# Retention in a streaming encoder step: queries times state in two rounded parts and three passes; one value buffer, queries and keys tile by tile in three slots

## The reference, cut to what matters

```python
def step(r, qkv):
    qc, kc, vc = qkv
    qf, kf, vf = qc.astype(F32), kc.astype(F32), vc.astype(F32)
    s = jnp.einsum('bihd,bjhd->bhij', qf, kf) * intra[None]
    o = jnp.einsum('bhij,bjhe->bihe', s, vf)
    o = o + jnp.einsum('bihd,bhde->bihe', qf, r) * q_dec
    r = r * c_dec + jnp.einsum('bjhd,bjhe->bhde', kf * k_dec, vf)
    return r, o.astype(vc.dtype)
...
o = head_norm(o, gn_g.reshape(RET_HEADS, RET_DV)).reshape(b, L, RET_VW) * jax.nn.silu(g)
return x + gate[:, None, :] * (o @ w_out), r
```

## Time and profile before

| | us |
|---|---|
| median of 3 runs (1730.53 to 1733.26) | 1731.53 |
| the profiled execution, its own time | 1732.81 |
| its span, first to last instruction | 1731.0 |

### The profile page before, as it was taken

How to read it: one execution, slowest core, us unless ns; L and a number is a source line. 1 busy time by engine, 2 the same in 40 slices (tenths; PEclk the granted TensorE clock), 3 DMA queues, 4 the chain that set the end, 5 groups by cost and what they waited for, 6 DMA issues and landing times.

```text
span 1731.0 us, 22378 instructions
## 1 busy us (share of the span) xinstructions
PE 1677.8 (97%) x8585; PEld 1344.3 (78%) x8585; DVE 766.0 (44%) x1588; ACT 559.6 (32%) x926; POOL 380.9 (22%) x501
## 2 busy tenths in 40 slices
PE   3999999999999999999999999999999999999998
PEld 2899997777876766667668888888788876888987
DVE  4664443212244454545543333665553106654442
ACT  4221121111133435434440223523322125444442
POOL 2111111211133334333322223414211010110000
PEclk7999999999999999999999999999999999999999
DMA  9545545563456767677663312222322726343201
GB/s 309 182 146 175 186 143 194 177 219 130 166 165 203 241 185 237 181 224 241 201 234 113 110 42 89 95 98 75 96 91 86 219 92 197 128 118 103 74 25 37
DMA packets 137004, 260.75 MB, mean 151 GB/s; under 512 B 16931, under 2 KB 60095, under 8 KB 136898
## 3 DMA queue, kind: packets, MB, share of 16 engines
q1 hardware_dynamic: 104114, 167.23, 30.6%
q0 software_dynamic: 32784, 92.08, 15.6%
HBM read 178.83 MB, written 80.43 MB: 150 GB/s over the span
## 4 chain that ended last, share of the span: by engine, by line
PE 84%; DVE 5%; issue 2%; ACT 2%; DMA 2%; POOL 1%; SPq 0%; DVEq 0%; POOLq 0%
PE trunk_ps L1120 34%; PE in_ps_o L537 12%; PE in_ps_o L533 11%; PE tail_ps L2040 6%; PE tail_ps L2031 4%; PE tail_ps L1998 3%; PE trunk_ps L1163 3%; PE trunk_ps L1147 3%; PE tail_ps L2008 2%; PE tail_ps L1966 1%; DVE room L1558 1%; PE in_ps_o L558 1%; PE trunk_ps L1158 1%; POOL room L1428 1%; PE trunk_ps L1223 1%
## 5 line engine op out<-in xcount | busy, mean ns | idle before, releaser
L1120 PE MATMUL trunk_ps<-w_hi,hT_hi 128*128 128x512 f32 x1008 | 412.3, 409 | 0.6 <-DVE w_lo L210 0.6
L1120 PE MATMUL trunk_ps<-w_hi,hT_lo 128*128 128x512 f32 x1008 | 399.3, 396 | 0.0
L1120 PE MATMUL trunk_ps<-w_lo,hT_hi 128*128 128x512 f32 x1008 | 398.0, 395 | 0.0
L1120 PEld LDWEIGHTS trunk_ps<-w_hi,hT_hi 128*128 128x128 f32 x1008 | 189.7, 188 | 60.7 <-issue 17.5
L1120 PEld LDWEIGHTS trunk_ps<-w_lo,hT_hi 128*128 128x128 f32 x1008 | 189.9, 188 | 48.1 <-issue 5.0
L1120 PEld LDWEIGHTS trunk_ps<-w_hi,hT_lo 128*128 128x128 f32 x1008 | 189.5, 188 | 46.3
L210 DVE TENSOR_TENSOR w_lo<-w_raw,w_hi 128x1024 fp32r<-128x1024 f32 x76 | 96.5, 1271 | 114.3 <-ACT w_hi L198 108.7
L533 PE MATMUL in_ps_o<-hT_hi,w_hi 128*128 128x384 f32 x384 | 130.6, 340 | 0.4 <-DVE hT_lo L664 0.4
L533 PE MATMUL in_ps_o<-hT_hi,w_lo 128*128 128x384 f32 x384 | 129.1, 336 | 0.0
L533 PE MATMUL in_ps_o<-hT_lo,w_hi 128*128 128x384 f32 x384 | 129.0, 336 | 0.0
L537 PE MATMUL in_ps_o<-w_hi,hT_hi 128*128 128x512 f32 x288 | 114.4, 397 | 0.0
(11 more groups left out here) (256 smaller groups left out, 2854.6 us busy)
## 6 DMA issues: line engine op xcount, KB each, us to landing
w_raw<-in_a_w_in SPq DMA_DIRECT2D x96, 256.0 KB, 3.4
room<-in_state_ret SPq DMA_DIRECT2D x64, 256.0 KB, 4.3
out_state_sample<-room POOLq DMA_DIRECT2D x64, 256.0 KB, 6.8
room<-in_b_ada_w SPq DMA_DIRECT2D x24, 512.0 KB, 6.7
scratch_qkT<-room POOLq DMA_DIRECT2D x48, 192.0 KB, 2.2
scratch_v_hi<-room POOLq DMA_DIRECT2D x36, 256.0 KB, 2.6
scratch_v_lo<-room POOLq DMA_DIRECT2D x36, 256.0 KB, 3.1
scratch_o<-room POOLq DMA_DIRECT2D x36, 256.0 KB, 3.4
```

Of the source, the lines that this page charges most:

```text
L1120: ins = pe.matmul(ps[:, bank, :], h[:, k, t * P:(t + 1) * P], w[:, (C0 + j) % 2, k, :], start=k + m == 0, stop=k == KT - 1 and m == 2)
```

## The change: what it does

1. The query-state product of tiles 1 to 7 is made of six fp32r matmuls (three for each half of the state) in place of two fp32 ones. Their operands are made one tile ahead: ACT rounds the state and the next tile's queries behind the scaling of the output, POOL makes the state's low part ahead of the gating, DVE the queries' low part behind the coefficients and ahead of `half_low` and `split_lo`.
2. Values have one buffer: POOL issues the load for tile n + 1 right after output n, ahead of the state's low part.
3. Queries and keys come tile by tile (256 KB each) into a ring of three slots, each freed by the scores and by the query's low part (or by the copy for the strips).
4. The semaphores of a few memory clears and of the last head's row loads are merged; buffers move.

```diff
-        qk = [at(9216, 4, NB3), at(11776, 4, NB3)]
+        qk = [at(9216 + 4 * P * i, 4, P) for i in range(3)]
...
+        def qk_landed(h, c):
+            g = score_no(h, c)
+            return qk_in[g % 3], 16 * (g // 3 + 1)
...
             def load_qk(g):
...
+                h, c = g // T, order[g % T]
+                if g >= 3:
+                    ph, pc = (g - 3) // T, order[(g - 3) % T]
+                    sp.wait_ge(scored, g - 2)
+                    if pc == SELF:
                         sp.wait_ge(qs_ready, ph + 1)
+                    elif pc:
+                        sp.wait_ge(q_split, 7 * ph + pc)
...
+                src = dr["qkT"][4 * h:4 * h + 4, :, c * P:(c + 1) * P].rearrange("a p t -> p a t")
+                sp.dma_start(qk[g % 3], src).then_inc(qk_in[g % 3], 16)
...
+                    if T * h + t + 4 < T * RH:
+                        load_qk(T * h + t + 4)
...
             def output(h, c):
...
                 if c:
-                    pe.wait_ge(state_new, n)
-                    q, _ = qk_of(h, c)
+                    pe.wait_ge(q_split, 7 * h + c)
+                    pe.wait_ge(state_split, 7 * h + c)
                     for a in range(2):
-                        ins = pe.matmul(ps[:, PS_O, :], q[:, a, :], state[:, a, :], start=False, stop=a == 1)
+                        for m, (q, r_) in enumerate(((q_hi, state_hi), (q_hi, state_lo), (q_lo, state_hi))):
+                            ins = pe.matmul(ps[:, PS_O, :], q[:, a, :], r_[:, a, :], start=False, stop=a == 1 and m == 2)
...
                     act.activation(o_t, ps[:, PS_STR if t == SELF else PS_O, :], ACT.Identity, bias=sc[:, 2:3], scale=sc[:, 1:2]).then_inc(o_scaled, 1)
+                    if t + 1 < PT:
+                        act.wait_ge(state_new, PT * h + t + 1)
+                        act.copy(state_hi[:, :, :], state[:, :, :]).then_inc(hi_made, 1)
+                        act.wait_ge(*qk_landed(h, t + 1))
+                        act.copy(q_hi, qk_of(h, t + 1)[0]).then_inc(hi_made, 1)
                     if t % 2 and t < 2 * SUBS:
...
             def load_v(n):
...
-                if n >= 2:
-                    ph, pc = divmod(n - 2, PT)
+                if n:
+                    ph, pc = divmod(n - 1, PT)
                     pool.wait_ge(o_done, ph * T + pc + 1)
...
+            def state_low(h, c):
+
+                pool.wait_ge(hi_made, 14 * h + 2 * c + 1)
+                pool.tensor_tensor(state_lo[:, :, :], state[:, :, :], state_hi[:, :, :].bitcast(F32), ALU.subtract).then_inc(state_split, 1)
...
+                    if t < PT and PT * h + t + 1 < RH * PT:
+                        load_v(PT * h + t + 1)
+                    if t + 1 < PT:
+                        state_low(h, t)
                     pool.wait_ge(g_evac, n + 1)
                     pool.wait_ge(o_scaled, n + 1)
                     pool.tensor_tensor(o_t, o_t, g_t[:, :], ALU.mult).then_inc(gated, 1)
...
-                    if t < PT and 8 * h + t + 2 < RH * PT:
-                        load_v(8 * h + t + 2)
...
+            def query_low(h, c):
+
+                dve.wait_ge(hi_made, 14 * h + 2 * c)
+                dve.tensor_tensor(q_lo, qk_of(h, c)[0], q_hi.bitcast(F32), ALU.subtract).then_inc(q_split, 1)
...
                     coefficients(n)
+                    if t + 1 < PT:
+                        query_low(h, t + 1)
                     if h == RH - 1:
                         half_low(t, 1)
```

More of the change, by code:

```diff
@@ L773, in trunk @@
         part = lambda o, n: pr.parts[:, o:o + n]
-        v_hi, v_lo = (part(o, 2 * DV).rearrange("p (a b) -> p a b", a=2) for o in (0, 2 * DV))
-        k_hi, k_lo = part(4 * DV, DK), part(4 * DV + DK, DK)
-        s_hi, s_lo = part(4 * DV + 2 * DK, P), part(4 * DV + 2 * DK + P, P)
+        v_hi, v_lo = part(0, DV), part(DV, DV)
+        k_hi, k_lo = part(2 * DV, DK), part(2 * DV + DK, DK)
+        s_hi, s_lo = part(2 * DV + 2 * DK, P), part(2 * DV + 2 * DK + P, P)
+        state_hi, state_lo = pr.state_hi, pr.state_lo
+        q_hi, q_lo = pr.q_parts[:, 0], pr.q_parts[:, 1]
         vs = at(6912, DV)
@@ L808, in trunk @@
         ps_t = ps[:, 4:8, :].rearrange("p (a b) c -> p a b c", a=2)
-        qk_in = [sem(f"qk_in{i}") for i in range(2)]
-        v_in = [sem(f"v_in{i}") for i in range(2)]
+        qk_in = [sem(f"qk_in{i}") for i in range(3)]
+        v_in, hi_made, q_split, state_split = sem("v_in"), sem("hi_made"), sem("q_split"), sem("state_split")
         parted = sem("parted")
@@ L815, in trunk @@
         o_stored = [sem(f"o_stored{i}") for i in range(2)]
-        orow_in = [sem(f"orow_in{i}") for i in range(2)]
         vs_in, cols_in, p_stored = sem("vs_in"), sem("cols_in"), sem("p_stored")
-        scored, decayed, s_ready, qs_clear, qs_ready = sem("scored"), sem("decayed"), sem("s_ready"), sem("qs_clear"), sem("qs_ready")
+        scored, decayed, s_ready, cleared, qs_ready = sem("scored"), sem("decayed"), sem("s_ready"), sem("cleared"), sem("qs_ready")
         upd, o_done, state_new, strips_done, strip_new = sem("upd"), sem("o_done"), sem("state_new"), sem("strips_done"), sem("strip_new")
@@ L892, in score_no @@
             return h * T + order.index(c)
[L894 to L897, removed]
+        def qk_landed(h, c):
+            g = score_no(h, c)
+            return qk_in[g % 3], 16 * (g // 3 + 1)
         def qk_of(h, c):
-            _, buf, at_ = portion_of(h, c)
-            cut = slice(at_ * P, (at_ + 1) * P)
-            return qk[buf][:, 0:2, cut], qk[buf][:, 2:4, cut]
+            slot = qk[score_no(h, c) % 3]
+            return slot[:, 0:2], slot[:, 2:4]
         def strip_tile(t):
@@ L967, in orow_load @@
                     sp.wait_ge(half_turned, 2 * t + half - 1)
[L968 removed]
+                sp.dma_start(orow[half], dr["o"][t * P:(t + 1) * P, half * CW:(half + 1) * CW]).then_inc(o_in[half], 16)
             def o_rows(i):
@@ L1195, in half_turn @@
             def half_turn(t, half):
-                pe.wait_ge(orow_in[half], 16 * (t + 1))
+                pe.wait_ge(o_in[half], 16 * (t + 1))
                 if t + half:
@@ L2305, in build @@
             under.enter_context(nc.sbuf_tensor("under_room", [P, 4096], F32))
-            pr.parts = under.enter_context(nc.sbuf_tensor("parts", [P, 4 * DV + 2 * DK + 2 * P], F32R))
+            pr.parts = under.enter_context(nc.sbuf_tensor("parts", [P, 2 * DV + 2 * DK + 2 * P], F32R))
+            pr.state_lo = under.enter_context(nc.sbuf_tensor("state_lo", [P, 2, DV], F32R))
+        with ExitStack() as under:
+            under.enter_context(nc.sbuf_tensor("under_queries", [P, 11776], F32))
+            pr.q_parts = under.enter_context(nc.sbuf_tensor("q_parts", [P, 2, 2, P], F32R))
+            pr.state_hi = under.enter_context(nc.sbuf_tensor("state_hi", [P, 2, DV], F32R))
         room = acts.enter_context(nc.sbuf_tensor("room", [P, ROOM], F32))
```

54 lines of the change are left out of this document (16 added, 38 removed).

## The result

| | before | changed kernel |
|---|---|---|
| median of 5 runs, us | 1731.53 (1728.71 to 1733.47) | 1804.26 (1800.35 to 1808.62) |
| profiled execution, us | 1732.81 | 1800.35 |
| its span, us | 1731.0 | 1798.5 |
| ratio of the medians, 95% interval | | 1.0424 [1.0400, 1.0448] |

What follows compares the result with a forecast made beforehand. TensorE, busy almost throughout, bounds the kernel; every second retention tile it waits for ACT, then DVE. -9.4 + 41.6 + 12 + 9.1 + 6 = +59 us on 1732.8 gave 1792, 1791 as a median; range 1752 to 1812.

Steps and rivals of the forecast that it cites:

- passes: Query-state product, tiles 1 to 7 of four heads: six rounded passes replace two fp32 matmuls, saving 9.4 us.
- splitting: Making high and low parts on ACT, POOL and DVE delays TensorE in retention: 41.6, 9.1 and 6 us.
- strips: Tiles 2, 4, 6 of four heads: later strips delay the update 3.0, 3.7 and 3.7 us, 41.6 in all.
- head 3: Tiles 3, 5, 7 of the last head: the query subtraction delays TensorE's turn 2.8 to 3.5 us, 9.1 in all.
- head starts: Tile 0 of heads 1 to 3: late scaling and splits hold the state product 2.0 us each, 6 in all.
- one value buffer: Tiles 3, 5, 7, heads 0 to 2: loads landing after 6.6 us stall the update 1.1, 1.1, 1.8: 12 us.
- query ring: SP's tile-by-tile query loads: slots are read over a tile later, so no wait of TensorE, taken as 0.
- The first rival: Retention stage: engines don't block each other, only ACT's 1.25 us reach the strips; +23 us, 1755; chance 0.15.
- The rival "faster": Retention stage: splits lie in idle time of ACT, DVE and POOL, TensorE keeps its 9.4 us; 1722; chance 0.03.
- the lower bound: Tiles 3, 5, 7: value loads landing after 4.3 us are hidden, the query's low part is next, 5 us.
- At nothing: Items priced at 0: copies' waits, POOL's order, the scaling-to-scaling loop, SP's query loads, the first value load.
- The forecast's bound for the ring: Query loads at their upper landing time: up to 2.5 us in 12 tiles, 30 more, 1821; chance 0.05.

Runs made afterwards that it cites:

- filled: Changed kernel plus unused matmuls where TensorE waits for strips, 14 per strip tile, 16 in head 3: 1785.42 us, 1.0315 of the kernel before.
- fp32_ring_up: fp32_product with the query ring's second and third load issued right behind the first: 1738.02 us, 1.0042 of the kernel before.
- ring_up: Changed kernel with SP's second and third query load right behind the first, ahead of weights and states: 1798.89 us, 1.0391 of the kernel before.
- query_first: Changed kernel with ACT's two copies swapped, queries first and state second: 1786.26 us, 1.0318 of the kernel before.
- fp32_product: Changed kernel with the product back in fp32 and no splitting operations; one value buffer and ring stay: 1744.18 us, 1.0077 of the kernel before.
- early: Changed kernel with ACT's copies ahead of the scaling, both low parts on DVE ahead of the weight split, none on POOL: 1735.77 us, 1.0026.
- state_low_dve: Changed kernel with the state's low part made by DVE behind the query's, not by POOL: 1761.01 us, 1.0174 of the kernel before.

## Why the prediction was right

By its terms, with the runs that price them:

| term | forecast, us | measured, us | from |
|---|---|---|---|
| passes | -9.4 | -9.2 | 28 x (1.73 - 1.40), the two chains |
| splitting, at full clock (strips 41.6, head 3 9.1, head starts 6) | +56.7 | +50.5 | 1804.26 - 1744.18 + 9.2 - 18.8 |
| clock after the waits | not in it | +18.8 (15.1 between the profiled executions) | 1804.26 - 1785.42 (filled) |
| one value buffer | +12 | about +7 | 1738.02 - 1731.09 (fp32_ring_up) |
| query ring | 0 | +5 to 6 | ring_up, fp32_ring_up |

The measured terms add up to 73 because they are differences along one row of kernels, each with another part left out; that is no proof of the single terms. The value buffer's was taken beside the fp32 product; in the changed kernel these waits lie partly behind those of the splitting, so only the sum of the two (57 or 58 for 69) is firm.

**The passes and the splitting.** Right nearly to the instruction. The state's low part on POOL lies at B+5.8 to 8.2 (forecast 5.84 to 8.31), the query's on DVE at B+6.0 to 8.4 (6.0 to 8.6), the update at B+12.5 to 12.6 in heads 0 to 2 (12.8), and `filled` gives the strip tiles' stall to 1 us in 37. The first rival, engines that don't block each other, is out: 2401 ns for an operation that takes 425 to 451 alone. The Trainium skill's rule holds for this too ("SBUF — State Buffer", Who interferes with whom: the ports that DVE and GpSimd share are an exclusive lock, and the order of issue decides who blocks). The forecast took the block in; without it the same sum gave 1755. The rival "faster" needed the weight split to reach DVE by B+5.70; it did so at B+7, and at B+8.4 behind the query subtraction. `query_first` adds what the forecast left out: without that subtraction in POOL's time the weight subtraction inherits the block.

**The clock.** This is the step that was missing. The forecast took matmuls behind a longer stall at their old durations. Before, no wait of TensorE in retention was over 2.0 us, and from 600 us on the clock stayed at 1.00. Now it stands for 3.3 to 4.2 us in nine of the twelve strip tiles, and each time it comes back to 1.2 GHz (granted clock 0.50). Behind the wait of 1.96 us in tile 2 it does so in heads 0 and 2, but not in head 1. The chain of head 3, tile 4, shows the price on the product (start, us, what):

```profile
889.62 2.09 PE trunk_ps L1183 x8
891.70 3.81 PE trunk_ps L1112 x9
...
900.47 5.60 PE trunk_ps L1112 x24
```

Nine matmuls take 0.42 us each; at full clock they follow at 0.23.

**The value buffer.** Mis-sized, and its mechanism with it. The loads land in 3.4 to 8.3 us, 4.2 in the median (6.1 before); the second load of each pair, for which 6.6 was taken from the earlier trace rows, in 4.5 (landing over all of them, then the median of that group):

```profile
DMA to landing us min/median/max: 3.4/4.2/8.3
...
parts<-scratch_v_lo POOLq DMA_DIRECT2D x32, 256.0 KB, 4.5
```

So in five of the nine tiles 3, 5 and 7 of heads 0 to 2 the update doesn't wait, and in four of these the query's low part is next, as the lower bound had it: in tile 5 of head 1 the state product starts at B+8.5, released by L1594 (from the chain; B is 665.65 there):

```profile
671.67 2.44 DVE q_parts L1594
...
674.15 1.67 PE trunk_ps L1154 x6
```

In the other four, three of them in head 0, the update waits 0.4 to 1.0 us; the profile names no releaser. The nine tiles cost 3.8 us net; the lower bound gave 1.7, the value taken 8.9. The longest wait of that kind is at a head's start: in tile 1 of head 2 the second load, issued at 720.7, lands 8.3 us later, and TensorE's update starts just then (in order of time; the profile names no releaser).

```profile
729.14 1.63 PE L1138 MATMUL trunk_ps<-parts 128*128 128x512 f32 x6 [2.59 <-issue]
```

By the Trainium skill's figure ("DMA: Bandwidth & Descriptors", Anatomy of one DMA) the estimate was 2.6 us; the smallest measured is 3.4.

**Head 3.** Mechanism right: TensorE's turn waits for the low half of the rows. In tiles 3, 5 and 7 it cost 10.8 net for 8.1. In the strip tiles I had only the strips' shift; there the same low half ends the wait, up to 4.2 us ahead of the strips, and the clock falls on top: 14.7 for 9.4, of which `filled` gives 5.4 back.

**Head starts.** Forecast 6 us; tile 1 of heads 1 to 3 together cost 1.8 net, 2.8 before passes, and that is the value load of head 2 (2.4 net). In heads 1 and 3 tile 1 costs -0.4 and -0.2, so the stall of 2.0 us each did not come. In tile 0 DVE, ahead of the scaling, waited for the store of the old state (3.23 us in head 1). That store (512 KB) now lands after 4.7 us in the median, 8.4 before, and all that DVE waits for it is 0.2 us once; so the copies start sooner than the earlier trace rows had them. Tile 0 of these heads looks 0.6 to 0.9 us shorter only because DVE comes 0.9 to 1.0 us later to the moments of the tile 8 before it; in `fp32_product` and `early`, where the store lands as soon, both tiles are unchanged.

**At nothing.** Wrong for the ring. The sum asked when a slot is read, a tile later, and not where its first loads stand: loads 2 and 3 are issued from 494.91 on, behind a quarter of a head's states and a part of the weights (SP's queue in order of time), and the score at 500.58 waits for one. Before, the first portion, with tiles 0, 1 and 8, stood ahead of all that.

```profile
491.82 1.87 SPq L946 DMA_DIRECT2D room<-in_state_ret  x4
493.73 1.02 SPq L176 DMA_DIRECT2D w_raw<-in_a_w_in  x2
494.91 0.95 SPq L922 DMA_DIRECT2D room<-scratch_qkT  x2
```

```profile
500.58 0.71 PE L1124 MATMUL trunk_ps<-room 128*128 128x128 f32 x4 [1.03 <-DMA room<-scratch_qkT]
```

The forecast's bound for the ring (30 us in 12 tiles) was for a wait in the steady state, which does not occur.

So the sum came out 13 us low: a clock of 19 and a ring of 5 to 6 were missing, and splitting and values together were 11 too high. Part of the error cancelled, so that the sum came this near is in part luck.

## What to carry to other kernels

An operation that idle engines have room for is free only in a place where nobody waits: the same subtractions cost 60 us behind the scaling and ahead of the weight split, and nothing in the scaling's own wait and behind the strips. When a DVE operation with two SBUF inputs is put beside one on POOL, count it with POOL's duration, and look at what is next on DVE, since a changed order only moves the block. When a change adds a stall of some microseconds to TensorE, price the clock behind it as well as the stall; and look at where the first load of a new ring stands in its queue.

## What the runs showed of the hardware

The granted clock fell to 0.50 behind all nine of TensorE's waits of 3.3 to 4.2 us in the tiles with strips, behind two of the three of 1.96 us, and in `state_low_dve` once behind 1.54 us. The product's matmuls then took 0.42 us each in place of 0.23. With unused matmuls in the same gaps it stayed at 1.00 in heads 1 and 2, and the whole ran 18.8 us faster, [1.0301, 1.0329] of the kernel before for [1.0400, 1.0448]. That the gate has these two levels and goes by what TensorE has lately done is also what the Trainium skill states ("TensorE: Matmul & The Clock Gate", Part 1: The HAM clock gate); here it was a fifth to a quarter of the whole loss (15.1 to 18.8 us of 73). The state's low part takes 2.37 us on POOL and 1.21 on DVE.
